# Zero matmuls ahead of the first weights, and the second weight block rounded between the x tiles of the first norm

## The reference

```
def rms_norm(x, w):
    xf = x.astype(jnp.float32)
    y = xf * lax.rsqrt(jnp.mean(xf * xf, axis=-1, keepdims=True) + NORM_EPS)
    return (y * w.astype(jnp.float32)).astype(x.dtype)

def gdn_shortconv_mixer(h, w_in, qkv_conv, a_log, dt_bias, o_norm, sc_conv, w_out):
    qkv, z, a, b, b_gate, c_gate, hs = jnp.split(h @ w_in, _split_points(sizes), axis=-1)
    qkv = jax.nn.silu(causal_dwconv(qkv, qkv_conv))
    ...
    g = -jnp.exp(a_log.astype(f32)) * jax.nn.softplus(a.astype(f32) + dt_bias.astype(f32))
    beta = jax.nn.sigmoid(b.astype(f32))
    ...
x = x + gdn_shortconv_mixer(rms_norm(x, mix_norm[0]), ...)
```

## Time and profile before

| | us |
|---|---|
| median of 3 runs | 2047.55 (2046.58 to 2051.38) |
| profiled execution, its own time | 2047.05 |
| its span, first to last instruction | 2045.2 |
| TensorE busy in the span | 2028.1 (99%) |
| VectorE, ScalarE, GpSimd busy | 1167.2, 1005.6, 727.0 |
| first real matmul starts | 7.57 |

### The profile page before, as it was taken

One profiled execution on the slowest core, in us unless ns is written; L12 is line 12 of the kernel. 1 busy time (PEld: TensorE's weight loads), 2 busy tenths in 40 slices (PEclk: granted clock), 3 DMA queues, 4 the chain that ended last, 5 costly groups with the idle time before them and its releaser, 6 DMA issues.

```text
span 2045.2 us, 30152 instructions
## 1 busy us (share of the span) xinstructions
PE 2028.1 (99%) x12180; PEld 1673.0 (82%) x12180; DVE 1167.2 (57%) x1983; ACT 1005.6 (49%) x1629; POOL 727.0 (36%) x316
## 2 busy tenths in 40 slices
PE   8999999999999999999999999999999999999999
PEld 6777788989888886778898898878788887878887
DVE  6875566665647157863656665667733334774331
ACT  7742464444436328874544343666743344765221
POOL 3342144434444631004434444434044443402443
PEclk9999999999999999999999999999999999999999
DMA  4432123332332430002333223222022222201222
GB/s 160 137 126 72 47 97 103 103 104 95 102 104 86 149 94 33 1 16 93 103 104 104 93 104 103 85 81 93 2 83 102 93 96 90 83 22 63 93 98 88
DMA packets 62728, 179.18 MB, mean 88 GB/s; under 512 B 17776, under 2 KB 18160, under 8 KB 62592
## 3 DMA queue, kind: packets, MB, share of 16 engines
q1 hardware_dynamic: 47600, 168.04, 24.1%
q10 hardware_dynamic: 14992, 9.22, 1.7%
HBM read 171.97 MB, written 3.70 MB: 86 GB/s over the span
## 4 chain that ended last, share of the span: by engine, by line
PE 97%; ACT 1%; DVE 1%; issue 0%; DMA 0%; POOL 0%; DVEq 0%; ACTq 0%
PE banks L869 23%; PE banks L870 22%; PE banks L871 22%; PE banks L975 4%; PE banks L974 4%; PE banks L973 4%; PE banks L1360 2%; PE banks L1326 2%; PE banks L1339 2%; PE banks L1449 1%; PE banks L1462 1%; PE banks L1434 1%; PE banks L920 1%; PE banks L1440 1%; PE banks L1042 1%; PE banks L1234 1%
## 5 line engine op out<-in xcount | busy, mean ns | idle before, releaser
L3105 POOL TENSOR_TENSOR w_lo<-raw,w_hi 128x1024 fp32r<-128x1024 f32 (+2 forms) x312 | 726.8, 2331 | 1301.8 <-ACT w_hi L1587 1301.7
L1587 ACT ACTIVATE w_hi<-raw 128x1024 fp32r<-128x1024 f32 (+2 forms) x312 | 317.6, 1018 | 490.2 <-PE banks L871 337.2
L869 PE MATMUL banks<-h_lo,w_hi 128*128 128x512 f32 (+1 forms) x992 | 400.7, 404 | 7.6 <-POOL w_lo L3105 7.6
L871 PE MATMUL banks<-h_hi,w_hi 128*128 128x512 f32 (+1 forms) x992 | 387.6, 391 | 0.0
L870 PE MATMUL banks<-h_hi,w_lo 128*128 128x512 f32 (+1 forms) x992 | 387.3, 390 | 0.0
L869 PE MATMUL banks<-a_lo,w_hi 128*128 128x512 f32 x768 | 304.0, 396 | 0.0
L871 PE MATMUL banks<-a_hi,w_hi 128*128 128x512 f32 x768 | 299.2, 390 | 0.0
L870 PE MATMUL banks<-a_hi,w_lo 128*128 128x512 f32 x768 | 299.2, 390 | 0.0
L2354 DVE TENSOR_TENSOR x<-x,banks 128x512 f32<-128x512 f32 x168 | 115.3, 686 | 213.5 <-PE banks L871 213.5
L869 PEld LDWEIGHTS banks<-h_lo,w_hi 128*128 128x128 f32 (+1 forms) x992 | 185.9, 187 | 54.1 <-issue 7.6
L870 PEld LDWEIGHTS banks<-h_hi,w_lo 128*128 128x128 f32 (+1 forms) x992 | 186.1, 188 | 41.9 <-issue 5.3
(11 more groups left out here) (422 smaller groups left out, 3726.1 us busy)
## 6 DMA issues: line engine op xcount, KB each, us to landing
raw<-in_weights SPq DMA_DIRECT2D x311, 512.0 KB, 3.2
x<-in_x SPq DMA_DIRECT2D x4, 512.0 KB, 5.7
AT<-row_dram ACTq DMA_DIRECT2D x4, 512.0 KB, 8.5
out<-x SPq DMA_DIRECT2D x8, 256.0 KB, 2.0
eg<-row_dram ACTq DMA_DIRECT2D x8, 128.0 KB, 3.1
phase<-in_phase ACTq DMA_DIRECT2D x1, 706.0 KB, 4.0
phase<-in_phase ACTq DMA_DIRECT2D x1, 704.0 KB, 4.0
ld_dram<-Ld ACTq DMA_DIRECT2D x1, 512.0 KB, 4.6
```

The costliest lines, as they stand in the source:

```text
L869: mm(out, w_hi, x_lo, start=first, stop=False)
L871: return mm(out, w_hi, x_hi, start=False, stop=last)
L1587: f(c.w_hi[:, b % RING, to], c.raw[:, b % RING, cols], ACT.Copy).then_inc(c.w_hi_ready, 1)
L3105: return nc.gpsimd.tensor_tensor(c.w_lo[:, slot, to], c.raw[:, slot, first:end], c.w_hi[:, slot, to].bitcast(F32), ALU.subtract)
```

## The change

Before the "ab" product TensorE waits for the first of VectorE's two clears and runs 15 matmuls of 512 columns on the zeros of X, read as 16-bit numbers, into bank 7, whose content nobody reads. VectorE clears X first and XT second. ScalarE rounds weight block 1 ahead of x tile 6 in the loop that makes h_hi, where it stood behind that loop. The norm's sum is issued inside the second GDN tile, which is TensorE's third product, after its second k step, where it stood behind the first GDN tile.

```
+WARM = 15
+NORM_SUM_AT = (1, 1)
...
+    idle = c.X[:, :, :].rearrange("p a b -> p (a b)").bitcast(BF16)
+    pe.wait_ge(c.x_clear, 1)
+    for _ in range(WARM):
+        mm(c.psum[7][:, :], idle[:, 0:P], idle[:, P:P + T], start=True, stop=True)
     gemm(("ab",), h_hi, h_lo, needs=parted("h", 0), width=AB_ROWS)
...
         def run(k):
+            if (t, k) == NORM_SUM_AT:
+                pe.wait_ge(c.common_loaded, 16)
+                norm_sum(0)
+                pe.wait_ge(c.phase0_loaded, 16)
...
         gemm(tile, h_hi, h_lo, beside=beside_tile(t))
-        if t == 0:
-            pe.wait_ge(c.common_loaded, 16)
-            norm_sum(0)
-            pe.wait_ge(c.phase0_loaded, 16)
...
     for k in range(KT):
-        if k == 2:
-            weights(0)
+        if k in (2, 6):
+            weights(k // 4)
         x_final(act, c, bank, 0, k)
         norm_hi(0, k)
-    weights(1)
     for k in range(KT):
...
+    v.memset(c.X[:, :, :], 0.0).then_inc(c.x_clear, 1)
     v.memset(c.XT[:, :, :], 0.0).then_inc(c.x_clear, 1)
-    v.memset(c.X[:, :, :], 0.0).then_inc(c.x_clear, 1)
```

## The result

The changed kernel takes 2052.32 us (median of 20 executions, 2050.59 to 2058.61), the kernel before 2047.9 us in the same comparison: a ratio of 1.0023, 95% interval 1.0016 to 1.0030. That is 4.4 us more at the median, inside the 0.3% that the prediction called no change. The forecast was 2050.2, its range 2046.8 to 2053.0.

What follows compares the result with a forecast made beforehand. TensorE bounds the kernel, up to L920 through the norm sum's issue and its fixed-latency chain. Tile 0 at 16.5, 5.47 for it and 1.36 for two k steps delay the sum 2.7: 2047.55 + 2.7 = 2050.2 us, range 2046.8 to 2053.0.

Steps and rivals of the forecast that it cites:

- no change: Whole kernel: differences within about 0.3%, 6.1 us, cannot be told apart; faster means below 2041.4, slower above 2053.7.
- The landing: ScalarE ahead of x tile 6: block 1 lands at 10.9, so ScalarE stands 1.3 us and w_lo gains nothing.
- The shared ports: VectorE's h_lo of tiles 6 and 7: held by GpSimd's subtraction for block 1, ready at 15.1 and 15.8.
- The zeros: Ahead of the ab product: 15 matmuls from about 1.55 to 7.1 raise the clock; first real matmul at 7.57.
- Rival (c): Ab product: zeros do not raise the clock; +0.2 us on the forecast, up to 2050.9; chance 0.06.
- The sum and the chain: Norm sum to L920: two k steps add 1.36 us, squares are not waited for, L920 keeps its distance.
- the two marks: Norm sum's start near 23.3 and the square's sum at L920 near 36.4 (20.64 and 33.75 before).
- its 2.7 us: Norm sum at 23.3 instead of 20.64, a delay of 2.7 us that stays to the kernel's end.
- the likeliest case: The forecast itself: VectorE held, zeros raise the clock, no later fall; 2050.2 us, chance 0.53.
- the term for the clock behind the stand: TensorE after its 3.4 us stand in the ab product: slow matmuls, 0 in the forecast, +2.1 us in rival (b).
- rival (b): After TensorE's 3.4 us stand in the ab product the clock falls back; +2.1 us, 2052.3; chance 0.13.

Runs made afterwards that it cites:

- e6: The changed kernel with GpSimd's subtraction for block 1 held back until h_lo of tile 7 is made; one execution, span 2048.5 us against 2045.2 before.
- e5: The changed kernel with 14 more zero matmuls between the ab product's k steps 5 and 6; 2051.36 us, ratio 1.0027 to the kernel before.
- e2: The changed kernel with block 1 and the norm sum back at their old places, so only the zeros; one execution, span 2047.5 us against 2045.2 before.
- e4: The changed kernel without zeros and with block 1 back behind the x tiles, so only the norm sum moved; one execution, span 2048.1 us against 2045.2.
- e10: The changed kernel with GpSimd's subtraction for block 4 held back until e_row is made; 2050.53 us, ratio 1.0018 to the kernel before.
- e9: The changed kernel once more, unaltered, in a second comparison; 2052.31 us, ratio 1.0027 to the kernel before.
- e7: The changed kernel with block 1 behind the x tiles, norm sum inside the first GDN tile, GpSimd's block 4 subtraction behind e_row; 2044.67 us, ratio 0.9993.
- e11: e7 without the zero matmuls; 2045.96 us, ratio 0.9992 to the kernel before.
- e12: e7 once more, unaltered; 2044.96 us, ratio 0.9984 to the kernel before.
- e3: The changed kernel without zeros, clears and norm sum as before, so only block 1 moved; one execution, span 2046.1 us against 2045.2 before.
- e1: The changed kernel with block 1 rounded behind all eight x tiles again, zeros and later norm sum kept; one execution, span 2045.3 us against 2045.2 before.

## Why the prediction came out as it did

**The landing.** Block 1 was expected at 10.9 and ScalarE's stand at 1.3 us: 11.02 and 1.24. Right, and the move bought nothing for w_lo, as said.

**The shared ports.** The rows of another stage priced the collision: h_lo of tile 6 ready at 15.1, tile 7 at 15.8. TensorE started k = 6 at 15.11, and the two h_lo ended at 15.71. e6 shows the cause: without GpSimd beside them they take 1.41 us. The Trainium skill (SBUF — State Buffer, "SBUF: two separate sides") states a rule for this: the pair of ports that GpSimd and VectorE share is an exclusive lock for a whole instruction, and no split of bandwidth. The trace agrees: GpSimd started first and ended at 14.51, and the first of the two h_lo, 0.7 us long by itself, was ready only for a matmul at 15.11.

**The zeros.** Start at 1.45, end at 7.14, first real matmuls 0.26 us apart at 7.51: as predicted (1.55, 7.1, 7.57). Rival (c), that they do not raise the clock, fell.

**The sum and the chain.** The squares were not waited for, two k steps cost 1.4 us, and L923 moved with the norm sum by the same amount in every run where it waits. With the clock kept up (e5) the two marks are 23.28 and 36.38 against 23.3 and 36.4. The mechanism and its 2.7 us were right.

**What was missing in the likeliest case** is the term for the clock behind the stand, which the forecast set to 0 and rival (b) at 2.1 us, with a chance of 0.13. It measured 1.6 us in one profiled execution of the changed kernel and 2.8 in the other. 2.7 + 1.6 is the 4.3 us that the profile shows, and the medians differ by 4.4 to 4.65. Rival (b) with its 2052.3 us described the median of 2052.32; that the two agree to some hundredths is luck, since its 2.1 us is neither of the two measured prices, and the single times hold other losses too. The step that failed is the weighing: a pause of 3.4 us, 3.7 times the longest one seen in the trace (0.91), was treated as probably harmless because "The trace has no pause to judge by". That reading was wrong. The trace of before has two stands of 0.63 and 0.91 us at 776 to 780, with TensorE busy for 2.45 of 4.00 us, and 0.57 granted from 780 to 784, in the lines shown under e2 to e4: far shorter stands were followed by a low clock, and this is the row that bore on (b). The Trainium skill (TensorE: Matmul & The Clock Gate, "HAM oscillation — how this bites in real kernels") warned that pauses between bursts of matmuls send the clock back, and the trace agrees, with 0.51 granted behind a stand of 3.24 us; e10, with none behind 3.0 us, shows that it need not happen. That the stand brings the fall is likely, with two of three profiled fronts against none of eleven, and not proved: e5 took the stand away in one profiled execution only, and a front can stay fast with the stand in place. How the term is shared among the 27 executions is not shown either, and e5 did not lower the median by what its front gained. What took e5's gain back is open; a fall behind the 1.9 us stand at L923, which e5 keeps and which cost 1.5 us in e4 and e6, is a candidate that its one profile does not show.

**The tail.** The collision of the two fetches near 105 us was not foreseen. It accounts for some 5 us in each of the two slowest profiled executions. Such times are more frequent with block 1 among the x tiles: counted from each kernel's own lowest time in its comparison, 9 of the 49 executions of the changed kernel (e9 included), e5 and e10 lie 5 us or more above it, none of the 33 of e7, e11 and e12, and 3 of 69 of before. That these are all the collision is not shown, and why it would come more often there is open. The distance hangs on when the store of the same 512 KB lands, 0.3 to 0.4 us later in e9 and e10 than elsewhere, for which no run gives a reason; it was 0.38 us in the first profile of the changed kernel, the same as before, and was not changed on purpose in any run. That the short distance makes the fetch slow is therefore read from 14 profiles, two with it and twelve without, and not from an experiment.

## What to carry to other kernels

Before moving a step ahead of others in an in-order engine, look up when its input lands: a wait that costs nothing at the old place, since the input arrives just then, becomes a stand for everything queued behind it at the new one. Moving work of GpSimd in time also moves it against VectorE's operations with two SBUF inputs, so the timelines of both belong side by side. And a pause of TensorE of some 3 us can have two prices, its own length and slow matmuls behind it (two of three profiles here). The granted clock behind the short pauses that a trace already has is the row to read before such a price is set to zero. The better version here came from leaving block 1 behind the x tiles and issuing the norm's sum earlier, inside the tile that runs when its input is ready, with the zeros kept.

## What the hardware showed that was not expected

The slow stretch at the start has no fixed length: the matmuls became fast at 12.0 us in the profile before, at 12.8 in e3, 13.3 in e4 and 13.6 in e11, with the same instructions from 7.6 to 7.7 on. The granted clock is given as 1.00 in this stretch although the matmuls are 0.43 us apart, so there the distance between starts is what tells the level. The fall at a stand has no fixed place either: in the changed kernel it came 1.2 us after the stand had ended, in e9 2.0 us after it had begun. Stands of 1.9 us were followed by 0.51 granted in two of six profiled executions (e4, e6), and not in the changed kernel, e1, e5 and e9; stands of 0.6 to 0.9 us with little work between them at 776 to 783 were followed by nothing (e1), by 4 us (before) or by 10 us (e2). Where two 512 KB transfers were issued 0.07 to 0.09 us apart, the first landed in 6.2 to 6.4 us; in the twelve profiles with 0.24 to 0.39 us between them it landed in 3.1 to 3.7.
